# Shift and scale of the first norm made by TensorE, a block of 128 channels at a time, among the products of the first chunk

## The chip, the cores and the metric

The kernel runs on one core of one Trainium2 chip. The metric is the device time of one execution in microseconds. Three runs of the kernel before gave 1728.87, 1730.22 and 1730.78 us; the median is 1730.22 us. The execution that was profiled took 1729.32 us, and its span from the first to the last instruction is 1727.5 us.

## The reference, cut to what matters

One decoder layer for 512 tokens of 1024 channels, all in f32. The change concerns only its first lines:

```
mod = (silu(c) @ w_ada + b_ada).reshape(6, 1024)        # c: 1024 values, w_ada: 1024 x 6144
shift_m, scale_m, gate_m, shift_f, scale_f, gate_f = mod
h = rms_norm(x, norm_mix_gain) * (1.0 + scale_m) + shift_m
proj = h @ w_in                                          # q | k | v | p, 4096 columns
```

`rms_norm` divides x by the root of the mean of its squares over the 1024 channels. What follows (causal pooling, differential attention, gates, output projection, a second norm, and an expert stage with product keys that reads two tables of 16384 x 1024) is not touched.

## The kernel before, in words

**Layout.** Channels stand on the 128 partitions, in KT = 8 blocks of 128; the 512 tokens stand in a row. Each projection is cut into chunks of 256 output columns (`CHUNKS`); a chunk gives two tiles (m = 0, 1) of 128 x 512. Every product is made of three fp32r matmuls (`mm3`, L559 to L561): weights and activations are split into a high and a low part, and high x high, high x low and low x high are added up in a bank. For chunk n, ScalarE writes the high part of the weights (`whi_make`, L884), VectorE or GpSimd subtracts to get the low part (`wlo_make` L1247, `wlo_first` L1849).

**Order of the work.** Each engine has its own program, written out by hand, and the engines meet at semaphores. SyncE issues the loads from one queue in the order of `STREAM`: first the eight megabytes of `w_ada` that belong to shift_m and scale_m, each into a buffer of its own (`ada_raw`, items 0 to 7), with x (`xT`, 2 MB) behind the first of them; then the chunks' weights (1 MB each) through a ring of three slots (`raw`), with the rest of `w_ada` woven in.

**The front, up to the first chunk.** VectorE multiplies and adds the pieces of `w_ada` with silu(c) into a row sum, `acc_ada`, for shift and for scale: 16 operations of 128 x 1024, two for each megabyte (`ada_chunk`, L1220 and L1222). Each partition then holds the partial sum of its own channels. TensorE adds over the partitions and turns the row into columns: eight matmuls with one moving column each (`ada_columns`, L583), once for shift and once for scale. VectorE adds the bias (`ada_finish`, L1234) and forms `scaleA`.

Beside this, ScalarE squares x (L902), TensorE sums the squares over the channels with eight matmuls against a matrix of ones (`mean`, L571), ScalarE takes the root (L895, after a load of its table) and VectorE the reciprocal (L1280).

Then for each block k VectorE writes `tmp` (L1310), ScalarE the high part of h (L908), VectorE the low part (L1289), and TensorE multiplies block k into both tiles of chunk 0 (the branch `n == 0`, L744 to L758); the low part of the weights of tile 1 is used in eight matmuls at the end (L755). Chunk 1 follows, and from there the chunks run one after the other.

**After the front.** The chunks run to about 550 us, the expert stage streams one table through TensorE and gathers rows from both to the end. All of it is started by the work before it; nothing is set by a clock.

Of the kernel before, what the change touches and what calls it, by code (L numbers as in the profile page):

```python
# [6 lines left out]
P = 128  # L7
# [96 lines left out]
ADA_BEFORE_X = 1  # L104
# [101 lines left out]
def layer(nc, consts, chans, rows, xT_d, pos_d, subk_d, ada_d, wdram, downT, down, up, x1d, gated, out):  # L206
# [4 lines left out]
    with ExitStack() as ctx:  # L211
# [19 lines left out]
        def small(name, shape, dt=f32):  # L231
# [37 lines left out]
                   for n, kb in enumerate((68, 76, 84, 92, 116, 124, 181, 189))]  # L269
# [114 lines left out]
        sq_ready = sem("sq_ready")  # L384
        mean_ready = sem("mean_ready")
# [170 lines left out]
        def _(pe):  # L556
# [137 lines left out]
            t = 0  # L694
            for n, (stage, c) in enumerate(CHUNKS):
                if n == 1:
                    pe.wait_ge(const_in, 16)
# [23 lines left out]
                if n >= QUERY_B:  # L721
                    raw_arrived(pe, AT["w", n])
                else:
                    pe.wait_ge(hi_ready, n + 1)
                    if n == 0:
                        pe.wait_ge(lo_half, 1)
                    else:
                        pe.wait_ge(lo_ready, n + 1)
# [15 lines left out]
                elif n == 0:  # L744
                    for k in range(KT):
                        pe.wait_ge(alo_ready, N_OP["norm1"] + k + 1)
                        last = mm3(bank[:, BANK[t], :], wh[:, k, 0:P], wl[:, k, 0:P], ah[:, k, :], al[:, k, :],
                                   k == 0, k == KT - 1)
                        if k == KT - 1:
                            last.then_inc(tile_ready, 1)  # L750
                        pe.matmul(bank[:, BANK[t + 1], :], wh[:, k, P:CH], ah[:, k, :], start=(k == 0), stop=False)
                        pe.matmul(bank[:, BANK[t + 1], :], wh[:, k, P:CH], al[:, k, :], start=False, stop=False)
                    pe.wait_ge(lo_ready, 1)
                    for k in range(KT):
                        last = pe.matmul(bank[:, BANK[t + 1], :], wl[:, k, P:CH], ah[:, k, :], start=False,  # L755
                                         stop=(k == KT - 1))
                    last.then_inc(tile_ready, 1)
                    t += 2  # L758
# [22 lines left out]
                else:  # L781
                    for m in range(2):
                        free_bank(t)
                        for k in range(KT):
# [92 lines left out]
        def _(act):  # L877
# [23 lines left out]
            for k in range(KT):  # L901
# [307 lines left out]
        def _(dve):  # L1209
# [28 lines left out]
            def wlo_make(n):  # L1238
# [3 lines left out]
                if n == 0:  # L1242
                    dve.tensor_tensor(wlo[:, 0, :, P:CH], raw_w(0)[:, :, P:CH], whi[:, 0].bitcast(f32)[:, :, P:CH],
                                      ALU.subtract).then_inc(lo_ready, 1)
                    dve.wait_ge(lo_half, 1)
                    return
# [56 lines left out]
            dve.drain()  # L1303

            dve.scalar_tensor_tensor(scaleA[:, :], modc[:, KT:2 * KT], 1.0, chan[:, K_GMIX:K_GMIX + KT],
                                     ALU.add, ALU.mult)
            dve.drain()
            for k in range(KT + 1):
                if k < KT:
                    dve.scalar_tensor_tensor(tmp1[:, k, :], xT[:, k, :], scaleA[:, k:k + 1], rms1[:, :],  # L1310
                                             ALU.mult, ALU.mult).then_inc(part_ready, 1)
                if k:
                    lo_part(hT_lo[:, k - 1, :], tmp1[:, k - 1, :], hT_hi[:, k - 1, :], k, modc[:, k - 1:k])
            dve.sem_inc(root_used, 1)
# [523 lines left out]
        def _(pool):  # L1838
# [132 lines left out]
```

## Time and profile before

| what | value |
|---|---|
| median of 3 runs | 1730.22 us |
| profiled execution | 1729.32 us, span 1727.5 us |
| TensorE (PE) busy | 1604.2 us, 93% of the span |
| its weight loads (PEld) | 1175.7 us, 68% |
| VectorE (DVE) busy | 1266.0 us, 73% |
| ScalarE (ACT), GpSimd (POOL) busy | 536.4 us, 675.1 us |
| mean granted clock of TensorE | 0.970 |

Busy time of an engine over the whole span says little about one stage. The change lies in the first 53 us, so the rows below are mostly of that stretch, taken from a timeline: start, duration, engine, line, operation, output and inputs, shape, count, and in brackets how long the engine had been idle and what released it. A matmul on full f32 operands leaves two records in the trace, one on fp32r operands leaves one. The granted clock is given as a share of 2.4 GHz: 1.00 or 0.50.

### The profile page before, as it was taken

To read this page: it belongs to the slowest core of one execution; us is meant where nothing else is said; L and a number is where in the kernel's file an instruction comes from. 1 tells how busy PE (TensorE), PEld (TensorE's weight loads), DVE (VectorE), ACT (ScalarE), POOL (GpSimd) and SP (SyncE) were. 2 spreads that over 40 slices of the span, in tenths; PEclk is the share of its full clock that TensorE was granted. 3 is DMA by queue.
4 is the path that set the end of the run, shared out by engine and by line. 5 is a ranking of instruction groups with operands and counts; after the bars stand their busy time and mean duration, and the time that the engine had idled before them with its cause. 6 is when DMAs were issued, how large, how long until landed. Compare 5 with 4: busy or idle time off the path is not lost.

```text
span 1727.5 us, 20418 instructions
## 1 busy us (share of the span) xinstructions
PE 1604.2 (93%) x6936; PEld 1175.7 (68%) x6936; DVE 1266.0 (73%) x2419; ACT 536.4 (31%) x1347; POOL 675.1 (39%) x590
## 2 busy tenths in 40 slices
PE   4998999998998999999977999998999998999963
PEld 2887877776886998888866988997444443444421
DVE  6776556778466687999996888999566665676687
ACT  3432245454623612111115888876000000000000
POOL 0000121110002604534575666666744544456464
PEclk8999999999999999999988999999999999999997
DMA  8424422235332438999998999999999999999997
GB/s 334 182 87 160 151 67 78 79 102 195 143 113 86 172 122 299 376 342 351 391 335 327 382 393 392 391 390 379 360 409 409 409 409 411 409 410 409 409 411 283
DMA packets 126280, 499.18 MB, mean 289 GB/s; under 512 B 15456, under 2 KB 15840, under 8 KB 115808
## 3 DMA queue, kind: packets, MB, share of 16 engines
q0 software_dynamic: 75776, 269.52, 40.3%
q1 hardware_dynamic: 50400, 228.35, 34.5%
q8 instruction: 56, 0.92, 0.2%
q14 instruction: 48, 0.39, 0.1%
HBM read 492.04 MB, written 4.72 MB: 288 GB/s over the span
## 4 chain that ended last, share of the span: by engine, by line
DVE 30%; DMA 29%; PE 25%; POOL 5%; issue 4%; ACT 3%; DVEq 3%; SPq 0%; ACTq 0%
DMA ring<-in_up,idx 22%; DVE ring L1587 9%; DMA ring<-in_down,idx 7%; PE bank L559 6%; PE bank L560 5%; PE bank L561 5%; POOL ring L1841 5%; PE bank L848 4%; DVE accum L1830 2%; DVE acc_ada L1222 2%; PE bank L835 1%; ACT whi L884 1%; DVE wlo L1247 1%; DVE hot L1694 1%; DVEq L1256 1%
## 5 line engine op out<-in xcount | busy, mean ns | idle before, releaser
L848 PE MATMUL bank<-h2T,stream 128*128 128x256 f32 x2048 | 457.4, 382 | 9.6 <-ACTq L1178 9.6
L861 PE MATMUL bank<-stream,wmat 128*128 128x512 f32 x1024 | 444.7, 597 | 11.5 <-DMA stream<-in_up 7.0
L1830 DVE SCALAR_TENSOR_TENSOR accum<-ring,share,accum 128x1024 f32<-128x1024 f32 x245 | 314.6, 1284 | 178.1 <-DMA ring<-in_up,idx 175.1
L1841 POOL DMA_INDIRECT ring<-in_down,idx x256 | 326.4, 1275 | 271.0 <-DVE pre L1587 185.3
L848 PEld LDWEIGHTS bank<-h2T,stream 128*128 128x128 f32 x2048 | 387.2, 192 | 60.7 <-issue 9.9
L861 PEld LDWEIGHTS bank<-stream,wmat 128*128 128x128 f32 x1024 | 196.1, 192 | 259.4 <-issue 246.9
L1841 POOL DMA_INDIRECT ring<-in_up,idx x256 | 274.9, 1074 | 230.8 <-DVE accum L1830 191.7
L1587 DVE CUSTOM_DVE_ANT_0 ring<-ring,h2row 128x1024 f32<-128x1024 f32 x256 | 307.7, 1220 | 40.0 <-DMA ring<-in_down,idx 36.1
L559 PE MATMUL bank<-hT_hi,whi 128*128 128x512 f32 (+1 forms) x504 | 190.1, 377 | 12.1 <-DVE hT_lo L1289 9.5
L561 PE MATMUL bank<-hT_hi,wlo 128*128 128x512 f32 (+1 forms) x504 | 185.1, 367 | 0.0
L560 PE MATMUL bank<-hT_lo,whi 128*128 128x512 f32 (+1 forms) x504 | 184.8, 367 | 0.0
L1856 POOL TENSOR_TENSOR wlo<-raw,whi 128x2048 fp32r<-128x2048 f32 x8 | 37.2, 4655 | 203.2 <-ACT whi L884 203.2
L559 PEld LDWEIGHTS bank<-hT_hi,whi 128*128 128x128 f32 x504 | 97.0, 192 | 27.4 <-issue 11.9
L1190 ACT ACTIVATE junk<-yrow 128x1024 f32<-128x1024 f32 x4 | 4.2, 1056 | 347.4 <-DVE yrow L1805 347.4
L1247 DVE TENSOR_TENSOR wlo<-raw,whi 128x2048 fp32r<-128x2048 f32 x36 | 82.5, 2291 | 39.4 <-ACT whi L884 38.3
L884 ACT ACTIVATE whi<-raw 128x2048 fp32r<-128x2048 f32 x45 | 86.0, 1912 | 75.6 <-PE bank L561 71.5
L561 PEld LDWEIGHTS bank<-hT_hi,wlo 128*128 128x128 f32 x504 | 96.7, 192 | 15.8
L1149 ACT ACTIVATE h2T<-h2T,gT,gneg 128x128 f32<-128x128 f32 x256 | 105.5, 482 | 5.0 <-issue 0.3
L560 PEld LDWEIGHTS bank<-hT_lo,whi 128*128 128x128 f32 x504 | 97.1, 193 | 14.1 <-issue 0.2
L1177 ACT ACTIVATE wmat<-bank 128x256 f32<-128x256 f32 (+21 forms) x128 | 42.1, 329 | 190.7 <-PE bank L848 190.6
L1870 POOL DMA_DIRECT2D q_rot<-q_raw x64 | 33.1, 524 | 134.7 <-ACT q_raw L984 134.4
L1144 ACT ACTIVATE h2T<-cst,ijT 128x128 f32<-128x128 f32 x256 | 81.8, 390 | 6.5
(228 smaller groups left out, 1833.6 us busy)
## 6 DMA issues: line engine op xcount, KB each, us to landing
stream<-in_downT SPq DMA_DIRECT2D x128, 512.0 KB, 6.7
stream<-in_up SPq DMA_DIRECT2D x128, 512.0 KB, 6.8
raw<-in_ada SPq DMA_DIRECT2D x16, 1024.0 KB, 4.9
raw<-in_w_query SPq DMA_DIRECT2D x16, 1024.0 KB, 4.9
ada_raw<-in_ada SPq DMA_DIRECT2D x8, 1024.0 KB, 16.5
raw<-in_w_xp SPq DMA_DIRECT2D x4, 1024.0 KB, 12.8
raw<-in_w_gateA SPq DMA_DIRECT2D x4, 1024.0 KB, 4.8
raw<-in_w_branchP SPq DMA_DIRECT2D x4, 1024.0 KB, 4.8
```

Source lines behind the costliest of these rows:

```text
L559: pe.matmul(dst, lhi, rhi, start=first, stop=False)
L560: pe.matmul(dst, lhi, rlo, start=False, stop=False)
L561: return pe.matmul(dst, llo, rhi, start=False, stop=last)
L848: last = pe.matmul(bank[:, 4 + i % 2, 0:DT], stream[:, i % RING, k * P:(k + 1) * P], h2T[:, k, GB * P:S], start=(k == 0), stop=(k == KT - 1))
L861: last = pe.matmul(bank[:, 2 * tb + half, :], wmat[:, i, tb * P:(tb + 1) * P], stream[:, (ET + i) % RING, half * S:(half + 1) * S], start= ...
L884: act.activation(whi[:, n % 2], raw_w(n), ACT.Copy).then_inc(hi_ready, 1)
L1144: act.activation(h2T[:, 4 * par + n, P:2 * P], cst[:, C_IOTA:C_IOTA + P], ACT.Abs, bias=ijT[:, b, 0, t0 + n:t0 + n + 1])
L1149: last = act.activation(h2T[:, 4 * par + n, P:2 * P], h2T[:, 4 * par + n, P:2 * P], ACT.Relu, bias=gT[:, b, t:t + 1], scale=gneg[:, b, t:t ...
L1247: dve.tensor_tensor(wlo[:, n % 2], raw_w(n), whi[:, n % 2].bitcast(f32), ALU.subtract)\
L1587: dve.tensor_tensor_reduce(out=ring[slot][:, :], in0=ring[slot][:, :], in1=h2row[:, b, :], scale=1.0, scalar=0.0, op0=ALU.mult, op1=ALU.ad ...
L1830: dve.scalar_tensor_tensor(accum[:, b, :], ring[slot][:, :], share[:, b, k:k + 1], accum[:, b, :], ALU.mult, ALU.add).then_inc(sum_done, 1)
L1841: pool.indirect_dma_start(out=ring[slot][:, :], out_offset=None, in_=table, in_offset=bass.IndirectOffsetOnAxis(ap=idx[:, b, k:k + 1], axi ...
```

## The change: what it does, and the diff

1. **Layout of the weights.** The part of `w_ada` for shift and scale is laid out by output block on the host: piece k holds, for the 128 channels of block k, all 1024 x 128 weights of shift and all of scale. Before, a piece held 256 input rows of one of the two.
2. **Loads.** x comes first, then the weights of chunk 0 (now in front of the eight pieces), then the pieces; the small constants come behind the weights of chunk 1. `ada_raw` lies at other addresses.
3. **Multiplication.** The 16 operations of VectorE and the 16 matmuls of `ada_columns` go. In their place TensorE makes each block in 16 matmuls with one moving column (`ada_block`: 8 for shift, 8 for scale), adding up in the bank. VectorE adds the bias for two columns and forms one column of `scaleA` (`ada_columns_in`).
4. **Order.** TensorE's order is written out in `FRONT`: blocks a0, a1, a2, then the product of block 0 (p0), a3, p1, and so on. A product is now 6 matmuls for both tiles (`first_product`), without the eight at the end.
5. **Squares.** ScalarE squares five blocks, VectorE three. VectorE adds them in pairs, and TensorE sums four blocks where it summed eight. The table for the root is loaded ahead by a small operation.
6. **Low parts.** GpSimd makes both halves of chunk 0's low weights and one half of chunk 1's; VectorE makes one half of chunk 1's.

```diff
+FRONT = ("a0", "a1", "a2", "p0", "a3", "p1", "a4", "p2", "a5", "p3", "a6", "p4", "a7", "p5", "p6", "p7")
+SQUARE_PAIRS = ((0, 1), (2, 3), (5, 6), (4, 7))
...
             sp.dma_start(chan[:, :], chans).then_inc(chan_in, 16)
+            sp.dma_start(xT[:, :, :], xT_d).then_inc(xT_in, 16)
+            sp.dma_start(raw_at(OUTSIDE), wdram["xp"][0]).then_inc(raw_in[0], 16)
             for n, item in enumerate(STREAM):
...
-                sp.dma_start(raw_at(n), src).then_inc(ada_in[n] if m < 0 else raw_in[m % RAW_SLOTS], 16)
-                if n == ADA_BEFORE_X - 1:
-                    sp.dma_start(xT[:, :, :], xT_d).then_inc(xT_in, 16)
-                if n == OUTSIDE:
+                if m:
+                    sp.dma_start(raw_at(n), src).then_inc(ada_in[n] if m < 0 else raw_in[m % RAW_SLOTS], 16)
+                if n == OUTSIDE + 1:
...
+            def ada_block(k):
+                raw_arrived(pe, k)
+                if k == 0:
+                    pe.wait_ge(cact_ready, 1)
+                if k >= 2:
+                    pe.wait_ge(cols_read, k - 1)
+                for sec in range(2):
+                    for kk in range(KT):
+                        last = pe.matmul(bank[:, 5 + 2 * (k % 2), 3 * P + sec:3 * P + sec + 1],
+                                         ada_raw[k][:, (2 * kk + sec) * P:(2 * kk + sec + 1) * P],
+                                         cact[:, kk:kk + 1], start=(kk == 0), stop=(kk == KT - 1))
+                last.then_inc(cols_ready, 1)
+
+            def first_product(k):
+                wh, wl, ah, al = whi[:, 0], wlo[:, 0], hT_hi, hT_lo
+                if k == 0:
+                    pe.wait_ge(hi_ready, 1)
+                pe.wait_ge(alo_ready, N_OP["norm1"] + k + 1)
+                for m in range(2):
+                    if k == 0:
+                        pe.wait_ge(lo_half, m + 1)
+                    last = mm3(bank[:, BANK[m], :], wh[:, k, m * P:(m + 1) * P], wl[:, k, m * P:(m + 1) * P],
+                               ah[:, k, :], al[:, k, :], k == 0, k == KT - 1)
...
             pe.wait_ge(ones_ready, 1)
-            pe.wait_ge(sq_ready, 8)
-            mean([sq1[:, k, :] for k in range(KT)])
-            ada_columns(0)
-            ada_columns(1)
+            for n, (k, _) in enumerate(SQUARE_PAIRS):
+                pe.wait_ge(pair_ready, n + 1)
+                last = pe.matmul(bank[:, 6, :], ones[:, :], sq1[:, k, :], start=(n == 0),
+                                 stop=(n == len(SQUARE_PAIRS) - 1))
+            last.then_inc(mean_ready, 1)
+            for what in FRONT:
+                (ada_block if what[0] == "a" else first_product)(int(what[1:]))
+            pe.sem_inc(ada_col, 2)
...
-            for k in range(KT):
+            for k in range(5):
                 act.activation(sq1[:, k, :], xT[:, k, :], ACT.Square).then_inc(sq_ready, 1)
             act.wait_ge(ones_ready, 1)
+            act.activation(lamt[:, 0:1], eps_t[:, :], ACT.Sqrt)
             root(0, 1.0 / D)
...
-            dve.wait_ge(cact_ready, 1)
-            for j in range(2):
-                for r in range(4):
-                    ada_chunk(j, r)
-            inverse_root(0)
-            ada_finish(0)
-            ada_finish(1)
+            dve.wait_ge(xT_in, 16)
+            for k in (5, 6, 7):
+                dve.tensor_tensor(sq1[:, k, :], xT[:, k, :], xT[:, k, :], ALU.mult)
+            dve.drain()
+            for n, (one, two) in enumerate(SQUARE_PAIRS):
+                dve.wait_ge(sq_ready, (2, 4, 4, 5)[n])
+                dve.tensor_tensor(sq1[:, one, :], sq1[:, one, :], sq1[:, two, :], ALU.add).then_inc(pair_ready, 1)
+            inverse_root(0)
+            def ada_columns_in(k):
...
+                dve.wait_ge(cols_ready, k + 1)
+                dve.tensor_tensor(both, bank[:, 5 + 2 * (k % 2), 3 * P:3 * P + 2], bias, ALU.add).then_inc(cols_read, 1)
+                dve.drain()
+                dve.scalar_tensor_tensor(scaleA[:, k:k + 1], modc[:, KT + k:KT + k + 1], 1.0,
+                                         chan[:, K_GMIX + k:K_GMIX + k + 1], ALU.add, ALU.mult)
...
             for k in range(KT + 1):
                 if k < KT:
+                    ada_columns_in(k)
                     dve.scalar_tensor_tensor(tmp1[:, k, :], xT[:, k, :], scaleA[:, k:k + 1], rms1[:, :],
                                              ALU.mult, ALU.mult).then_inc(part_ready, 1)
                 if k:
                     lo_part(hT_lo[:, k - 1, :], tmp1[:, k - 1, :], hT_hi[:, k - 1, :], k, modc[:, k - 1:k])
...
-                pool.wait_ge(hi_ready, 1)
-                pool.tensor_tensor(wlo[:, 0, :, 0:P], raw_w(0)[:, :, 0:P], whi[:, 0].bitcast(f32)[:, :, 0:P],
-                                   ALU.subtract).then_inc(lo_half, 1)
+                for n, m in ((0, 0), (0, 1), (1, 1)):
+                    pool.wait_ge(hi_ready, n + 1)
+                    half = slice(m * P, (m + 1) * P)
+                    pool.tensor_tensor(wlo[:, n, :, half], raw_w(n)[:, :, half], whi[:, n].bitcast(f32)[:, :, half],
+                                       ALU.subtract).then_inc(lo_half, 1)
```

## Rows read from the trace of the kernel before

**Rows 1.** The page: span, and TensorE's busy tenths in 40 slices.

```profile
span 1727.5 us, 20418 instructions
PE   4998999998998999999977999998999998999963
```

**Rows 2.** Timeline of all engines, start of the program up to x and weights.

```profile
6.71 0.75 DVE L1220 TENSOR_SCALAR acc_ada<-ada_raw,cact 128x1024 f32<-128x1024 f32 x1 [5.69 <-DMA ada_raw<-in_ada]
11.53 4.27 ACT L902 ACTIVATE sq<-xT 128x512 f32<-128x512 f32 x8 [8.82 <-DMA xT<-in_xT]
14.01 8.08 DVE L1222 SCALAR_TENSOR_TENSOR acc_ada<-ada_raw,cact,acc_ada 128x1024 f32<-128x1024 f32 x6 [5.18 <-DMA ada_raw<-in_ada]
...
26.98 0.69 ACT L895 ACTIVATE rms<-bank,eps_t 128x512 f32<-128x512 f32 x1
31.42 1.91 ACT L884 ACTIVATE whi<-raw 128x2048 fp32r<-128x2048 f32 x1 [3.76 <-DMA raw<-in_w_xp]
32.60 3.35 DVE L1280 RECIPROCAL rms<-rms 128x512 f32<-128x512 f32 x1
33.41 2.36 POOL L1849 TENSOR_TENSOR wlo<-raw,whi 128x1024 fp32r<-128x1024 f32 x1 [32.96 <-ACT whi L884]
```

**Rows 3.** Timeline of TensorE alone, from its first matmul to chunk 1.

```profile
15.94 9.66 PE L571 MATMUL bank<-sq,ones 128*128 128x512 f32 x16 [15.94 <-ACT sq L902]
25.43 1.84 PE L583 MATMUL bank<-ones,acc_ada 128*128 128x1 f32 x16
32.57 3.58 PE L583 MATMUL bank<-ones,acc_ada 128*128 128x1 f32 x16 [5.29 <-DVEq L1227]
39.14 0.77 PE L559 MATMUL bank<-hT_hi,whi 128*128 128x512 f32 x1 [3.00 <-DVE hT_lo L1289]
39.70 0.63 PE L560 MATMUL bank<-hT_lo,whi 128*128 128x512 f32 x1
...
44.82 0.47 PE L751 MATMUL bank<-hT_hi,whi 128*128 128x512 f32 x1
...
52.85 0.39 PE L559 MATMUL bank<-hT_hi,whi 128*128 128x512 f32 x1
```

**Rows 4.** Timeline of the weight loads of the mean and of the one-column matmuls.

```profile
16.93 0.34 PEld L571 LDWEIGHTS bank<-sq,ones 128*128 128x128 f32 x1 [0.52 <-issue]
17.78 0.34 PEld L571 LDWEIGHTS bank<-sq,ones 128*128 128x128 f32 x1 [0.52 <-issue]
...
21.14 0.19 PEld L571 LDWEIGHTS bank<-sq,ones 128*128 128x128 f32 x1 [0.47 <-issue]
...
25.43 1.75 PEld L583 LDWEIGHTS bank<-ones,acc_ada 128*128 128x128 f32 x15 [0.24 <-issue]
32.57 3.49 PEld L583 LDWEIGHTS bank<-ones,acc_ada 128*128 128x128 f32 x16 [5.38 <-DVEq L1227]
```

**Rows 5.** Stretches: length, then busy us of PE, PEld, DVE, ACT, POOL; PEclk; DMA share; GB/s.

```profile
27.00:28.00 1.00, 0.28 (x3) 0.19 (x2) 0.93 (x2) 0.67 (x1) 0.00 (x0) 0.95 0.99 410
44.00:45.00 1.00, 1.00 (x4) 0.81 (x3) 1.00 (x3) 0.40 (x2) 0.00 (x0) 0.51 0.00 0
414.00:416.00 2.00, 2.00 (x20) 1.96 (x19) 1.91 (x3) 0.48 (x1) 0.00 (x0) 1.00 0.93 385
417.00:418.00 1.00, 0.00 (x0) 0.00 (x0) 1.00 (x1) 0.35 (x1) 0.00 (x0) 0.51 0.00 0
1680.00:1682.00 2.00, 0.30 (x1) 0.00 (x0) 1.83 (x3) 0.00 (x0) 1.70 (x2) 1.00 1.02 408
```

**Rows 6.** DVE groups of 60 to 140 us: busy, mean ns, idle before.

```profile
L1379 DVE TENSOR_TENSOR pool_w<-xpT 128x512 f32<-128x512 f32 x8 | 5.5, 690 | 0.6
```

**Rows 7.** What TensorE waited for from 52 to 700 us: total, times, longest.

```profile
PE bank L620 <- DVE comb L1417: 6.5, 9, 1.9
PE bank L559 <- DVE hT_lo L1289: 6.5, 1, 6.5
PE bank L559 <- ACT mergedP L1085: 2.4, 1, 2.4
```

More of the change, by code:

```diff
@@ L268, in layer @@
         ada_raw = [place(f"ada_raw{n}", [P, 2 * D], f32, kb)
-                   for n, kb in enumerate((68, 76, 84, 92, 116, 124, 181, 189))]
+                   for n, kb in enumerate((44, 60, 116, 124, 148, 181, 189, 197))]
         raw = place("raw", [P, RAW_SLOTS, KT * CH], f32, 12)
@@ L384, in layer @@
         sq_ready = sem("sq_ready")
+        pair_ready = sem("pair_ready")
+        cols_ready = sem("cols_ready")
+        cols_read = sem("cols_read")
         mean_ready = sem("mean_ready")
@@ L585, in ada_columns @@
                 last.then_inc(ada_col, 1)
-            pe.wait_ge(ones_ready, 1)
-            pe.wait_ge(sq_ready, 8)
-            mean([sq1[:, k, :] for k in range(KT)])
-            ada_columns(0)
-            ada_columns(1)
+            def ada_block(k):
[20 more added lines that the diff above has]
+                               ah[:, k, :], al[:, k, :], k == 0, k == KT - 1)
+                    if k == KT - 1:
+                        last.then_inc(tile_ready, 1)
+            pe.wait_ge(ones_ready, 1)
+            for n, (k, _) in enumerate(SQUARE_PAIRS):
[6 more added lines that the diff above has]
+            pe.sem_inc(ada_col, 2)
             ada_before = {}
@@ L692, in score @@
                 return t + 1
-            t = 0
+            t = 2
             for n, (stage, c) in enumerate(CHUNKS):
+                if n == 0:
+                    continue
                 if n == 1:
@@ L743, in _ @@
                             t += 1
-                elif n == 0:
-                    for k in range(KT):
[L746 to L758, printed above, removed]
                 elif stage == "v":
@@ L783, in _ @@
                         free_bank(t)
+                        if n == 1 and m == 1:
+                            pe.wait_ge(lo_half, 3)
                         for k in range(KT):
@@ L1242, in wlo_make @@
                 if n == 0:
-                    dve.tensor_tensor(wlo[:, 0, :, P:CH], raw_w(0)[:, :, P:CH], whi[:, 0].bitcast(f32)[:, :, P:CH],
+                    dve.wait_ge(lo_half, 2)
+                    dve.sem_inc(lo_ready, 1)
+                    return
+                if n == 1:
+                    dve.tensor_tensor(wlo[:, 1, :, 0:P], raw_w(1)[:, :, 0:P], whi[:, 1].bitcast(f32)[:, :, 0:P],
                                       ALU.subtract).then_inc(lo_ready, 1)
-                    dve.wait_ge(lo_half, 1)
+                    dve.wait_ge(lo_half, 3)
                     return
@@ L1295, in _ @@
             dve.sem_inc(ones_ready, 1)
-            dve.wait_ge(cact_ready, 1)
-            for j in range(2):
-                for r in range(4):
-                    ada_chunk(j, r)
-            inverse_root(0)
-            ada_finish(0)
-            ada_finish(1)
[L1303 to L1307, printed above, removed]
+            dve.wait_ge(xT_in, 16)
[7 more added lines that the diff above has]
+            def ada_columns_in(k):
+                both = modc[:, 0:2 * KT].rearrange("p (j k) -> p j k", k=KT)[:, :, k]
+                bias = chan[:, K_BADA:K_BADA + 2 * KT].rearrange("p (j k) -> p j k", k=KT)[:, :, k]
+                dve.wait_ge(cols_ready, k + 1)
[3 more added lines that the diff above has]
+                                         chan[:, K_GMIX + k:K_GMIX + k + 1], ALU.add, ALU.mult)
+                dve.drain()
+            dve.wait_ge(cact_ready, 1)
             for k in range(KT + 1):
                 if k < KT:
+                    ada_columns_in(k)
                     dve.scalar_tensor_tensor(tmp1[:, k, :], xT[:, k, :], scaleA[:, k:k + 1], rms1[:, :],
@@ L1313, in _ @@
                     lo_part(hT_lo[:, k - 1, :], tmp1[:, k - 1, :], hT_hi[:, k - 1, :], k, modc[:, k - 1:k])
+            dve.sem_inc(ada_acc, 2)
+            dve.sem_inc(ada_done, 2)
             dve.sem_inc(root_used, 1)
@@ L1945 @@
         "subk": np.ascontiguousarray(a["peer_sub_keys"][0].transpose(2, 0, 1)),
-        "ada": np.ascontiguousarray(a["w_ada"][0].reshape(4, 2, P, 6, D).transpose(3, 0, 2, 1, 4)
-                                    .reshape(6, 4, P, 2 * D)),
+        "ada": np.ascontiguousarray(np.concatenate([
+            a["w_ada"][0][:, :2 * D].reshape(KT, P, 2, KT, P).transpose(3, 1, 0, 2, 4).reshape(2, 4, P, 2 * D),
+            a["w_ada"][0][:, 2 * D:].reshape(4, 2, P, 4, D).transpose(3, 0, 2, 1, 4).reshape(4, 4, P, 2 * D)])),
         "w_xp": chunks(w_in[:, 3 * D:]), "w_q": chunks(w_in[:, :D]), "w_k": chunks(w_in[:, D:2 * D]),
```

7 lines of the change are left out of this document (1 added, 6 removed).

## The prediction

> **What bounds the kernel now.** I read the page first, for the span of 1727.5 us and the busy tenths of TensorE [rows 1]. After the first of the 40 slices they are mostly 8 or 9, so a front that ends later pushes a full TensorE ahead of it. Then I read what TensorE waits for between 52 and 700 us: single stalls of 6.5 and 2.4 us and a few short ones [rows 7], all on work that itself follows from earlier work. Nothing there waits for an absolute time, so I let a shift of the end of the front reach the end of the kernel one to one.
>
> Then the timeline of the first 53 us. The first megabyte of `w_ada` is there at 6.71, x (2 MB behind it) at 11.53, the next megabyte at 14.01, and the eleventh and last, the weights of chunk 0, at 31.42 [rows 2]: 2.4 to 2.5 us for each megabyte. VectorE is the bound before the first product: it waits 5.18 us for the second megabyte, then works without a gap from 14.01 to 32.5 through the rest of its 16 row operations, and takes 3.35 us for the reciprocal from 32.60 [rows 2]. TensorE has only the mean (9.66 us from 15.94) and two batches of eight one-column matmuls (1.84 us at 25.43, 3.58 us at 32.57); the first product starts at 39.14 and chunk 1 at 52.85 [rows 3]. The reader should see that VectorE works and TensorE is nearly empty, and, just as important, what the few one-column matmuls cost. The point to compare is the start of chunk 1, 52.85 us.
>
> **The change, part by part.**
>
> *Loads.* Only the order changes. x is first and is there at 11.53 less one megabyte of 2.4, about 9.1; the chunk's weights about 11.5; piece k about 14.0 + 2.5 k; the last about 31.4, where the eleventh megabyte lands now [rows 2]. These arrivals are no bound if TensorE comes to each piece later, which it does below.
>
> *Squares and mean.* ScalarE does eight squares in 4.27 us [rows 2], so five take 2.7 us: 9.1 to 11.8. VectorE squares three blocks beside it and adds a pair. The nearest row is 0.69 us for a 128 x 512 addition [rows 6], so the first pair is ready at 9.1 + 4 x 0.7 + drains, about 12.0. TensorE then needs four f32 matmuls of two records each. At the low level records start 0.85 us apart (16.93, 17.78) and the loads shorten at 21.14, 5.2 us after the first matmul [rows 3, 4]: that is TensorE at 1.2 GHz, then at 2.4 GHz. Eight records take 6.8 us at the low level; with the rise after 5.2 us I take 6.0, to 18.0. The other pairs are added in 0.7 us each, beneath matmuls of 1.7 us. The root takes 0.69 and the reciprocal 3.35 [rows 2]; with the table loaded ahead, VectorE has the reciprocal at about 22.4. Bounds: 17.3 to 18.8 for the end of the mean.
>
> *High and low parts of chunk 0.* Its weights are there, so ScalarE's 1.91 us and GpSimd's two halves of 2.36 us [rows 2] end near 25.5, beneath the blocks a0 to a2.
>
> *The blocks on TensorE.* This is the large term. `ada_block` issues 16 matmuls of f32, 128 x 128 weights, one moving column, the same form as L583. Eight of those took 3.58 us at the low level and 1.84 us at the high one, and their weight loads fill that time: 3.49 us for 16 and 1.75 for 15 [rows 3, 4]. So the single column costs nothing and the weights everything. The change has 8 blocks x 16 = 128 matmuls, sixteen such batches: 16 x 3.49 = 55.8 us at 1.2 GHz, or 16 x 1.75 = 28.0 us at 2.4 GHz. Before, TensorE had two batches. The 16 operations that VectorE loses had run beside an idle TensorE; the work now lies on the engine that also has the products.
>
> The Trainium skill ("TensorE: Matmul & The Clock Gate", section on LDWEIGHTS) gives a load as its columns over 1.2 GHz, whatever the array's clock: an estimate from it is 107 ns for 128 columns, 256 records, 27 us in all. The trace agrees at the high level and disagrees at the low one, where a load takes 218 ns; by the page the slow case below would not exist.
>
> *The products.* 8 x 6 = 48 fp32r matmuls, as many as now. They start 0.43 us apart at the low level: the twelve between 39.70 and 44.82 [rows 3]. At the high level a record on fp32r takes half of this, 0.22 to 0.23. So 20.5 us or 10.9 us.
>
> *The clock.* All 77 us of this can go at either level. The granted clock fell near 27.9, right after the first batch of one-column matmuls, with TensorE idle only since 27.27, and near 417 after a stretch from 414 to 416 in which TensorE was busy for all 2.00 us, 1.84 of it such a batch [rows 3, 5]. Near the end of the kernel it stayed at 1.00 though TensorE was busy 0.30 of 2.00 us, with matmuls 512 wide around the gap [rows 5]. So the batches do not hold the clock up as wide matmuls do. In the changed kernel a0, a1 and a2 follow each other for over 10 us with one column each. I expect the fall about 3 us after the mean (27.9 - 25.4 in one case, 417 - 414.1 in the other). The rises of the trace came 5.2 us after dense matmuls began (15.94 to 21.14) and 5.8 us (39.14 to 44.98) [rows 3, 4, 5]; the product blocks, 2.56 us each between blocks of 7.0, are shorter than both, so I take no rise among them.
>
> *Waits that come in.* a2 to a7 wait until VectorE has read the block two before. Behind that wait stands all of TensorE; but VectorE is free from 22.4 and reads a block within 0.3 us, while each block lasts at least 3.5, so it costs nothing; if VectorE were late by a block it would cost up to 3 us once. A product k waits for the low part k, which stands behind `ada_columns_in(k + 1)` on VectorE, and so behind block a(k+1). In `FRONT` each product up to p5 has that block well before it. After a7, p6 and p7 need 2.2 and 2.8 us of VectorE and ScalarE (now 3.0 from the end of the one-column matmuls, 36.15, to the first product [rows 3]). At the low level p5 and p6 cover this; at the high level 0.9 us shows. Chunk 1 needs its high part (1.91) and half a subtraction behind the last high part of h: a7 + 5.3 us. The last block's products at the low level end at a7 + 6.5 and cover it.
>
> *The sum.* Mean ends 18.0. Blocks 55.8 and products 20.5 at the low level give 94.3. Minus 3.0, since about 3 us at the high level do 6 us of low work. Minus 1.25 at the end: p5, p6 and p7 are 7.7 us of dense matmuls, the clock rises after 5.2, and the remaining 2.5 takes half. That gives 90.0 for the start of chunk 1 against 52.85: +37.2 us. VectorE, next in line behind, ends its last low part 2.8 us after a7, 3.6 us before TensorE ends, and has 2.3 us less of subtractions behind it, so it is no later than TensorE. The profiled execution would go from 1729.32 to 1766.5; that execution is 0.9 us under the median of the runs, so the forecast is 1767.
>
> Bounds of this case: with 5 us at the high level after the mean, and rises in the mean and after p5 that come 1.5 us sooner than those of the trace (my allowance), 17.3 + 76.3 - 5.0 - 2.0 = 86.6, or +33.8. With neither and the mean wholly at the low level, 18.8 + 76.3 = 95.1, or +42.3. So 1763 to 1773.
>
> **The rivals.**
>
> *The clock stays high (B).* TensorE has no gap from the mean on. For it: the low level came each time with at least 0.6 us of idle TensorE as well. Against it: rows 5 as read above. Time: 18.0 + 28.0 + 5 x 1.36 = 52.8 at the end of a7, + 5.3 to chunk 1, 58.1: +5.3 us, 1735.5. The Trainium skill (the same page, "HAM oscillation") lays a fall to gaps of idle time between matmuls; by that rule there is none here and B holds. The trace agrees only in that the idle stretch and the batch came together.
>
> *The clock comes and goes (D).* The five product blocks between, or a favourable alternation, lift it for part of the way: between a quarter and three quarters of the 32 us between B and A, +13 to +29, say 1751. For it: a product block fills a good part of the time that a rise took at the least. Against it: both rises of the rows came more than 5 us into dense work, and a product block lasts 2.56.
>
> *Not slower: the arrival decides (C).* If a block took TensorE only one record for each matmul, eight would cost 0.9 us: 18.0 + 14.4 + 6.8 + 5.3 = 44.5, or -8.4 us, 1722; the last piece's arrival at 31.4 is the floor beneath it. The point from which it decides is a batch of eight under 1.4 us at the high level: then the front ends before 52.85. For it: VectorE's 18 us row work really goes, and x is there 2.4 us sooner. Against it: the batch has the same shape as L583, 16 records, 1.84 us at its best [rows 3].
>
> **How the numbers follow.** A 0.72, D 0.10, B 0.12, C 0.03, and 0.03 for a shift that is swallowed later by a stall that I let pass [rows 7]. The likeliest is A: 1767. The range runs from 1748, which takes in most of D, to 1774, the upper bound of A with a little for the unmeasured VectorE squares; it leaves out B and C. About 0.2% (3.5 us) is what a measurement can tell from no change. B at +5.3 still counts as slower, so slower is A, D and B with a part of the rest, 0.95; same 0.02; faster 0.03.
>
> **What would show it.** In the profile after: one-column matmuls, 256 records, beginning near 18 us; a granted clock of 0.50 from about 21 until the last products; a batch of 32 records in 7.0 us each; the products between in 2.6 us; `ada_raw` never waited for; chunk 1 near 90 us; everything behind it as before, moved by 37 us. I am wrong if the clock stays at 1.00 through a1 and a2 (then B), if a block takes clearly less than 3.5 us (then C), or if the end of the kernel does not move with chunk 1.

## The result, and the profile after

| | before | changed |
|---|---|---|
| median | 1729.59 us (4 runs, 1728.87 to 1730.78) | 1764.63 us (4 runs, 1759.33 to 1767.09) |
| ratio | | 1.0198, 95% interval 1.0171 to 1.0225 |
| profiled execution | 1729.32 us, span 1727.5 | 1767.09 us, span 1765.3 |
| start of chunk 1 | 52.85 us | 87.38 us |

The kernel became 35 us slower. The forecast was 1767, with a range from 1748 to 1774.

The timeline of TensorE in the changed kernel shows the front whole (L623 is the mean, L601 the blocks, L564 to L566 the products; start, duration, count; in brackets how long it was idle). It answers to [rows 3].

```profile
11.75 5.96 PE L623 MATMUL bank<-sq,ones 128*128 128x512 f32 x8 [11.75 <-DVE sq L1330]
17.55 18.44 PE L601 MATMUL bank<-cact,ada_raw 128*128 128x1 f32 x96
35.84 0.77 PE L564 MATMUL bank<-hT_hi,whi 128*128 128x512 f32 x1
...
38.55 6.82 PE L601 MATMUL bank<-cact,ada_raw 128*128 128x1 f32 x32
45.23 0.77 PE L564 MATMUL bank<-hT_hi,whi 128*128 128x512 f32 x1
...
64.00 0.77 PE L564 MATMUL bank<-hT_hi,whi 128*128 128x512 f32 x1
...
66.71 4.04 PE L601 MATMUL bank<-cact,ada_raw 128*128 128x1 f32 x32
70.61 0.48 PE L564 MATMUL bank<-hT_hi,whi 128*128 128x512 f32 x1
...
73.02 6.83 PE L601 MATMUL bank<-cact,ada_raw 128*128 128x1 f32 x32
79.70 0.77 PE L564 MATMUL bank<-hT_hi,whi 128*128 128x512 f32 x1
...
87.38 0.47 PE L564 MATMUL bank<-hT_hi,whi 128*128 128x512 f32 x1 [1.01 <-DVE wlo L1271]
```

From 11.75 to 86.4 us TensorE has no gap. A block of 32 records starts its product 6.68 us later (38.55 to 45.23): 0.209 us a record. One block, a6, takes 3.90 (66.71 to 70.61). The stretches show why; they answer to [rows 5] (length, then busy us of PE, PEld, DVE, ACT, POOL, the granted clock, DMA share, GB/s).

```profile
17.00:19.00 2.00, 2.00 (x16) 1.64 (x15) 0.53 (x1) 1.25 (x2) 0.00 (x0) 1.00 0.99 418
19.00:21.00 2.00, 2.00 (x15) 2.00 (x14) 2.00 (x1) 1.23 (x1) 0.69 (x1) 0.69 1.03 430
21.00:23.00 2.00, 2.00 (x11) 2.00 (x11) 1.28 (x3) 0.00 (x0) 2.00 (x2) 0.50 1.00 418
...
66.00:68.00 2.00, 2.00 (x12) 1.81 (x10) 0.09 (x1) 0.18 (x1) 0.00 (x0) 0.61 0.00 0
68.00:70.00 2.00, 2.00 (x20) 2.00 (x19) 0.00 (x0) 0.00 (x0) 0.00 (x0) 1.00 0.00 0
```

With TensorE busy throughout, the clock falls near 19.8, two microseconds into the one-column matmuls, and stays at 1.2 GHz. It rises near 67.6, 0.9 us into a6 and behind the wide product block p3, is high for the rest of a6, falls again at 71.0 in p4, and rises near 84.6, within the last products.

VectorE, the bound before, now waits 43.2 us for TensorE's blocks:

```profile
DVE modc L1338 <- PE bank L601: 43.2, 8, 7.5
```

Behind the front the shift is carried on. The first row is the table stage on TensorE of the changed kernel, the second the stage behind it, the third that same stage in the kernel before (first and last start are the two numbers after the durations):

```profile
L871 PE MATMUL bank<-h2T,stream x2048: 379/379/767, 709.5 to 1237.6; 128*128 128x256 f32 x187
L884 PE MATMUL bank<-stream,wmat x1024: 592/592/1222, 1244.4 to 1694.7; 128*128 128x512 f32 x171
```

```profile
L861 PE MATMUL bank<-stream,wmat x1024: 592/592/1222, 1207.1 to 1658.2; 128*128 128x512 f32 x171
```

The table stage started at 676.5 before and starts at 709.5 now: +33.0. The stage behind it starts at 1244.4 instead of 1207.1: +37.3. Between them lie 534.9 us instead of 530.6. In the profiles of the experiments below, whose code there is the same, this distance was 526.7 us (e6) to 536.6 us (e8), so I count the 4.3 us to that spread and not to the change.

### The profile page after: what moved, and what is told of

Same layout as the page of the kernel before. It is cut to its first block, busy times and chain, and to the rows that moved or that the text cites. A ratio compares the mean times of both kernels' runs of the same rounds, so it can differ in the third digit from the quotient of the medians.

```text
span 1765.3 us, 20862 instructions
## 1 busy us (share of the span) xinstructions
PE 1649.4 (93%) x7152; PEld 1220.3 (69%) x7152; DVE 1254.0 (71%) x2422; ACT 535.9 (30%) x1345; POOL 669.3 (38%) x592
## 4 chain that ended last, share of the span: by engine, by line
DMA 31%; DVE 29%; PE 24%; POOL 5%; issue 4%; ACT 4%; DVEq 3%; ACTq 0%; SPq 0%
DMA ring<-in_up,idx 21%; DMA ring<-in_down,idx 9%; DVE ring L1627 9%; PE bank L564 5%; POOL ring L1881 5%; PE bank L565 5%; PE bank L566 5%; PE bank L601 3%; DVE accum L1870 2%; PE bank L871 1%; ACT whi L907 1%; DVE wlo L1275 1%; DVE hot L1734 1%; DVEq L1284 1%; DVE att_max L1442 1%
## 5 line engine op out<-in xcount | busy, mean ns | idle before, releaser
L1881 POOL DMA_INDIRECT ring<-in_down,idx x256 | 319.7, 1249 | 281.3 <-DVE pre L1627 196.3
L1881 POOL DMA_INDIRECT ring<-in_up,idx x256 | 271.2, 1059 | 237.8 <-DVE accum L1870 199.1
L564 PE MATMUL bank<-hT_hi,whi 128*128 128x512 f32 (+1 forms) x512 | 196.4, 384 | 10.1 <-DVE hT_lo L1317 6.5
L565 PE MATMUL bank<-hT_lo,whi 128*128 128x512 f32 (+1 forms) x512 | 190.7, 372 | 0.0
L566 PE MATMUL bank<-hT_hi,wlo 128*128 128x512 f32 (+1 forms) x512 | 190.7, 372 | 0.0
L564 PEld LDWEIGHTS bank<-hT_hi,whi 128*128 128x128 f32 x512 | 100.0, 195 | 26.2 <-issue 10.3
L566 PEld LDWEIGHTS bank<-hT_hi,wlo 128*128 128x128 f32 x512 | 99.9, 195 | 16.6
```

What stands on the lines that cost most here:

```text
L564: pe.matmul(dst, lhi, rhi, start=first, stop=False)
L565: pe.matmul(dst, lhi, rlo, start=False, stop=False)
L566: return pe.matmul(dst, llo, rhi, start=False, stop=last)
L1881: pool.indirect_dma_start(out=ring[slot][:, :], out_offset=None, in_=table, in_offset=bass.IndirectOffsetOnAxis(ap=idx[:, b, k:k + 1], axi ...
```

## The experiments

My theory was that two things make the loss: the blocks put 256 weight loads on TensorE's path, and one-column matmuls let its clock fall, which doubles that price. The rivals were that the order and its waits make it, and that the low level alone does. Ratios are to the kernel before, run on the same chip in the same job.

### e1: the weights move instead of the one column

```diff
-                for sec in range(2):
-                    for kk in range(KT):
-                        last = pe.matmul(bank[:, 5 + 2 * (k % 2), 3 * P + sec:3 * P + sec + 1],
-                                         ada_raw[k][:, (2 * kk + sec) * P:(2 * kk + sec + 1) * P],
-                                         cact[:, kk:kk + 1], start=(kk == 0), stop=(kk == KT - 1))
+                for kk in range(KT):
+                    last = pe.matmul(bank[:, 5 + 2 * (k % 2), 0:2 * P], rep[:, kk, :],
+                                     ada_raw[k][:, 2 * kk * P:2 * (kk + 1) * P],
+                                     start=(kk == 0), stop=(kk == KT - 1))
...
```

`rep` is silu(c), each value repeated over 128 columns by VectorE. VectorE also picks the wanted columns out of the bank for each block, with a product and a sum over the columns.

> The changed kernel with operands swapped in the blocks: silu(c) of one block of 128 inputs, repeated over 128 columns, is the stationary operand and the weights move, 256 columns at once (8 matmuls a block in place of 16); VectorE picks the columns out with the identity. TensorE's passes are as many as before: 16 records of 256 columns a block. Theory 1 (the one-column form lets the clock fall, and the level makes most of the loss): blocks take about 3.4 us each, the clock stays at 1.00 through the front, chunk 1 starts near 58 to 59 us instead of 87.4, and the kernel takes 1735 to 1739 us. Rival (the new order and its waits make the loss): blocks may be shorter but chunk 1 stays near 85 us and the time near 1764 us.

Measured: 1739.52 us, ratio 1.0060 (1.0041 to 1.0079). Timeline of TensorE and two long stretches of it:

```profile
17.44 10.52 PE L603 MATMUL bank<-ada_raw,rep 128*128 128x256 f32 x48
28.88 0.47 PE L567 MATMUL bank<-hT_hi,whi 128*128 128x512 f32 x1 [0.92 <-issue]
...
30.34 3.62 PE L603 MATMUL bank<-ada_raw,rep 128*128 128x256 f32 x16
33.60 0.58 PE L567 MATMUL bank<-hT_hi,whi 128*128 128x512 f32 x1
...
56.31 0.50 PE L567 MATMUL bank<-hT_hi,whi 128*128 128x512 f32 x1 [1.61 <-DVE hT_lo L1319]
...
61.82 0.47 PE L567 MATMUL bank<-hT_hi,whi 128*128 128x512 f32 x1 [2.46 <-DVE wlo L1273]
```

```profile
18.00:36.00 18.00, 17.08 (x79) 14.56 (x78) 13.76 (x23) 4.29 (x5) 4.66 (x2) 1.00 1.02 417
36.00:54.00 18.00, 18.00 (x83) 15.51 (x83) 9.21 (x22) 2.89 (x4) 0.00 (x0) 1.00 0.08 32
```

The same sums in the same order, with wide moving operands: the clock is 1.00 in both stretches, a block's product starts 3.26 us after the block (30.34 to 33.60) in place of 6.68, and chunk 1 starts 25.6 us sooner than in the changed kernel. The order and its waits are still there, so they do not make the 35 us. The new form is also a little cheaper by itself: the rows of e3 put a one-column block at the high level at 3.43 us (an estimate, 32 x 0.107), so about 1.4 us of the 25.6 are the form and not the clock. Chunk 1 is 3 us later than I expected. TensorE, now faster, waits three times: 0.92 us before p0, 1.61 before p6, and 2.46 before chunk 1, the last for the reason that e6 shows.

### e2: all blocks first, then all products

```diff
-FRONT = ("a0", "a1", "a2", "p0", "a3", "p1", "a4", "p2", "a5", "p3", "a6", "p4", "a7", "p5", "p6", "p7")
+FRONT = ("a0", "a1", "a2", "a3", "a4", "a5", "a6", "a7", "p0", "p1", "p2", "p3", "p4", "p5", "p6", "p7")
```

> The changed kernel with all eight blocks first and all eight products behind them. The work on TensorE is the same. Theory 1 (level of the clock): the blocks run at 218 ns a load, the products are one dense stretch of 20.5 us at the low level in which the clock rises after some 5 us, so they take about 13 us; chunk 1 starts at 84 to 86 us, 1760 to 1764 us in all. Rival (interleaving hides work that would show otherwise): chunk 1 gets later, by the chain of VectorE and ScalarE that no longer runs between blocks, 5 us or more.

Measured: 1759.87 us, ratio 1.0172 (1.0133 to 1.0211).

```profile
17.64 52.50 PE L601 MATMUL bank<-cact,ada_raw 128*128 128x1 f32 x256
70.00 0.77 PE L564 MATMUL bank<-hT_hi,whi 128*128 128x512 f32 x1
...
74.41 0.47 PE L565 MATMUL bank<-hT_lo,whi 128*128 128x512 f32 x1
...
83.15 0.39 PE L564 MATMUL bank<-hT_hi,whi 128*128 128x512 f32 x1
```

The 256 records take 52.4 us on end. The dense products lift the clock 4.4 us after they begin, and chunk 1 starts at 83.15, with no wait of TensorE before it. The rival, that interleaving hides work, falls. Whether the order is worth anything is open: the changed kernel starts chunk 1 at 87.38 in one execution and at 81.68 in another (e9), on both sides of 83.15, and the intervals of the times overlap. It is in any case not the 35 us.

### e3: most of the sum for shift left out

```diff
-                    for kk in range(KT):
+                    for kk in range(KT if sec else 1):
...
```

> The changed kernel with seven of the eight matmuls left out of the sum for shift in each block (the sum for scale is whole): 9 matmuls a block instead of 16. Theory 1 (weight loads at 0.22 us a record set the front): 56 matmuls of two records less are 24 us at the low level; the product blocks are a larger part, so the clock may rise more often; chunk 1 near 60 us or earlier, total 1733 to 1740 us. Rival (waits set the front): less than 10 us gained.

Measured: 1738.83 us, ratio 1.0056 (1.0034 to 1.0078). The kernel leaves out seven eighths of the sum for shift: a block is 9 matmuls, 18 records.

```profile
30.93 2.31 PE L601 MATMUL bank<-cact,ada_raw 128*128 128x1 f32 x18
33.10 0.48 PE L564 MATMUL bank<-hT_hi,whi 128*128 128x512 f32 x1
...
34.57 2.07 PE L601 MATMUL bank<-cact,ada_raw 128*128 128x1 f32 x18
36.50 0.47 PE L564 MATMUL bank<-hT_hi,whi 128*128 128x512 f32 x1
...
54.32 0.47 PE L564 MATMUL bank<-hT_hi,whi 128*128 128x512 f32 x1 [2.48 <-DVE wlo L1271]
```

```profile
34.00:50.00 16.00, 15.49 (x105) 13.82 (x104) 8.99 (x20) 4.76 (x6) 0.00 (x0) 1.00 0.22 85
```

Chunk 1 starts 33 us sooner than in the changed kernel, more than the 24 us of loads taken out at the low level: with shorter blocks the clock comes back near 31.5 us and stays at 1.00 through the alternation, though the blocks still have one moving column. A block's product starts 1.93 us after the block (34.57 to 36.50): 0.107 us a record, the price of this form at the high level. The total, with routing computed from other values, gained less than the front (26 us), and I do not read more from it.

### e5: the rest of the change alone

Squares, pairs, table and the order of the loads as in the change; shift and scale as row operations of VectorE, as before.

```diff
             dve.sem_inc(ones_ready, 1)
+            dve.wait_ge(xT_in, 16)
+            for k in (5, 6, 7):
+                dve.tensor_tensor(sq1[:, k, :], xT[:, k, :], xT[:, k, :], ALU.mult)
...
             dve.wait_ge(cact_ready, 1)
             for j in range(2):
                 for r in range(4):
                     ada_chunk(j, r)
...
```

> The kernel before with only the other parts of the change: x and the weights of chunk 0 loaded first, squares shared by ScalarE and VectorE and added in pairs, table loaded ahead; shift and scale stay row operations of VectorE. Theory 1 (these parts are worth nothing by themselves since VectorE is the bound): VectorE has 4.4 us more of squares before the row operations and they start near 13.5 us, end near 35, chunk 1 at 54 to 56 us, total +1 to +3 us over the kernel before. Rival (the earlier x and mean bring something of their own): faster than before.

Measured: 1735.50 us, ratio 1.0043 (1.0028 to 1.0058). TensorE, then one row of VectorE:

```profile
37.08 3.58 PE L585 MATMUL bank<-ones,acc_ada 128*128 128x1 f32 x16 [6.80 <-DVEq L1233]
43.65 0.77 PE L561 MATMUL bank<-hT_hi,whi 128*128 128x512 f32 x1 [3.00 <-DVE hT_lo L1295]
...
56.51 0.47 PE L561 MATMUL bank<-hT_hi,whi 128*128 128x512 f32 x1
```

```profile
16.42 10.19 DVE L1228 SCALAR_TENSOR_TENSOR acc_ada<-ada_raw,cact,acc_ada 128x1024 f32<-128x1024 f32 x6 [0.27 <-DMA ada_raw<-in_ada]
```

The second batch of columns starts at 37.08 instead of 32.57 and chunk 1 at 56.51: 3.7 us later. The rival falls: an earlier x and an earlier mean bring nothing while VectorE's row operations set the end. I had not expected 2.1 us of it: six row operations take 10.19 us where they took 8.08 [rows 2]. One of them lasts 3.40 us instead of 1.28, while GpSimd makes its half of the low weights (20.48 to 22.82), which in the kernel before lay beside the reciprocal; e6 comes back to it. The timed loss, 5 to 10 us by the interval, is more than the front shows; the profiled execution was the fastest of ten (1730.6). What the others lose beyond the front is open.

### e4: the kernel before with TensorE kept at work

```diff
             ada_columns(0)
+            for _ in range(WARM_A):
+                pe.matmul(bank[:, 4, :], ones[:, :], sq1[:, 0, :], start=True, stop=True)
             ada_columns(1)
+            for _ in range(WARM_B):
+                pe.matmul(bank[:, 4, :], ones[:, :], sq1[:, 0, :], start=True, stop=True)
```

`WARM_A` is 6 and `WARM_B` is 3.

> The kernel before with nine wide f32 matmuls on TensorE whose result nobody reads: six behind the first batch of one-column matmuls, three behind the second. Theory 1: they hold the clock at 1.00 from 27 us on, the second batch takes 1.84 instead of 3.58 us and the first products start 0.23 us apart, but VectorE (reciprocal to 35.9, then 1.33 us for each block) sets the pace, so chunk 1 starts only 0.5 to 1 us earlier and the total does not change measurably. Rival (the low clock in the front of the kernel before costs its 5 us in full): 3 to 4.6 us faster.

Measured: 1729.33 us, ratio 0.9992 (0.9975 to 1.0010).

```profile
32.57 1.84 PE L584 MATMUL bank<-ones,acc_ada 128*128 128x1 f32 x16
34.27 2.82 PE L596 MATMUL bank<-sq,ones 128*128 128x512 f32 x6
...
51.75 0.47 PE L560 MATMUL bank<-hT_hi,whi 128*128 128x512 f32 x1 [0.64 <-DVE wlo L1252]
```

Wide matmuls between the batches hold the clock (1.00 from 18 to 54 us), the second batch takes 1.84 us in place of 3.58 [rows 3], and chunk 1 gains 1.1 us. So a low level costs almost nothing where VectorE is the bound. It cost some 25 us in the changed kernel (worked out behind the experiments) because the work had been moved onto the engine whose clock it lowers. Neither cause alone makes the 35 us.

### e6: chunk 1's low weights by VectorE alone

```diff
-                for n, m in ((0, 0), (0, 1), (1, 1)):
+                for n, m in ((0, 0), (0, 1)):
...
-                    dve.tensor_tensor(wlo[:, 1, :, 0:P], raw_w(1)[:, :, 0:P], whi[:, 1].bitcast(f32)[:, :, 0:P],
-                                      ALU.subtract).then_inc(lo_ready, 1)
-                    dve.wait_ge(lo_half, 3)
+                    dve.tensor_tensor(wlo[:, 1], raw_w(1), whi[:, 1].bitcast(f32), ALU.subtract).then_inc(lo_ready, 1)
...
```

> The changed kernel with the low part of chunk 1's weights made by VectorE alone (2048 columns, one instruction) instead of half by GpSimd and half by VectorE. In the changed kernel VectorE's half takes 3.44 us where the same shape took 1.22 before, and ends 1.1 us after GpSimd's half of 2.39. Theory 1 (VectorE's subtraction of two operands waits for the whole GpSimd instruction beside it): alone it takes 2.29 us, TensorE's wait of 1.0 us before chunk 1 goes. Rival (the time is set by something else in that place, such as the load of the weights): it takes more than 3 us again and the wait stays.

Measured: a single execution, 1759.15 us, which is too little to tell a gain in the total. The first two rows are from the changed kernel (VectorE's half, GpSimd's half), the third is VectorE's whole in e6.

```profile
83.79 3.44 DVE L1271 TENSOR_TENSOR wlo<-raw,whi 128x1024 fp32r<-128x1024 f32 x1 [0.72 <-ACT whi L907]
```

```profile
83.76 2.39 POOL L1891 TENSOR_TENSOR wlo<-raw,whi 128x1024 fp32r<-128x1024 f32 x1 [58.81 <-ACT whi L907]
```

```profile
84.01 2.29 DVE L1269 TENSOR_TENSOR wlo<-raw,whi 128x2048 fp32r<-128x2048 f32 x1 [0.71 <-ACT whi L905]
```

Both halves are issued together. VectorE's lasts until 87.23, 1.08 us after GpSimd's is over at 86.15: about its own length (the shape took 1.22 before). Alone, VectorE makes the whole in 2.29, and TensorE's wait before chunk 1 is gone. The two did not share, one waited for the other. The Trainium skill says so ("SBUF — State Buffer", section on the two separate sides): GpSimd and a VectorE operation with two SBUF inputs take the shared ports in turn, each for its whole instruction. The trace agrees, with 3.44 us for 1.22.

It shows in other places too. In the changed kernel GpSimd's first two halves run from 20.31 to 24.95, and an operation of VectorE on 128 x 1 elements, 0.16 us for every other block, lasts until they are over:

```profile
22.70 2.27 DVE L1340 SCALAR_TENSOR_TENSOR scaleA<-modc,chan 128x1 f32<-128x1 f32 x1
```

There it costs nothing, since TensorE is busy until 35.84. In e1 and e7 the like operation takes 1.98 us, VectorE works without a gap from there to the first low part of h, and TensorE stands idle for 0.92 us before p0; without the delay that idle time would not be there, by the times of these rows, but no run took it out.

### e7: e1 without the end of the front

ScalarE makes chunk 1's high part behind block 4; VectorE makes its low part between blocks, GpSimd none of it:

```diff
+                if k == 4:
+                    whi_make(1)
...
+                if k in (6, 7):
+                    dve.wait_ge(hi_ready, 2)
+                    half = slice((k - 6) * P, (k - 5) * P)
+                    dve.tensor_tensor(wlo[:, 1, :, half], raw_w(1)[:, :, half], whi[:, 1].bitcast(f32)[:, :, half],
+                                      ALU.subtract)
...
```

> e1 (weights moving, clock high) with the split of chunk 1's weights taken out of the end of the front: ScalarE makes the high part behind block 4, VectorE makes the low part in two halves behind blocks 5 and 6, GpSimd has no part of it. Theory 1 (with a high clock only TensorE's work is left: 27.3 us of blocks and 10.9 us of products behind the mean): chunk 1 starts at 58 to 59 us, with no wait ahead of it, 2.5 to 3.5 us earlier than in e1, and the kernel is 5 to 8 us slower than before. Rival (VectorE, which now has 2.4 us more between blocks, holds the products up): chunk 1 at 60 us or later.

Measured: 1736.21 us, ratio 1.0027 (1.0010 to 1.0044). Timeline of TensorE:

```profile
56.30 0.50 PE L567 MATMUL bank<-hT_hi,whi 128*128 128x512 f32 x1 [1.61 <-DVE hT_lo L1317]
...
59.60 0.39 PE L567 MATMUL bank<-hT_hi,whi 128*128 128x512 f32 x1
```

Chunk 1 starts at 59.60, directly behind the last product, 2.2 us sooner than in e1. That is less than the least I expected (2.5), and between my theory (58 to 59) and the rival (60 or later): the waits of 0.92 us before p0 and 1.61 before p6 are still there, as in e1. So the +6.8 us in the front are the blocks' price at the high clock with 2.5 us of idle TensorE in it.

### e8: rows and wide blocks mixed

Blocks 0 and 3 by VectorE in rows, the rest as in e7; four banks in turn for the blocks, and an order with more blocks ahead (a0 to a4 before p0).

```diff
+BY_ROWS = (0, 3)
...
+            def ada_rows(k):
+                n = BY_ROWS.index(k)
+                raw_arrived(dve, k)
+                acc = sq1[:, 2 * n + 1, 0:2 * P]
+                for kk in range(KT):
+                    src = ada_raw[k][:, 2 * kk * P:2 * (kk + 1) * P]
+                    if kk == 0:
+                        dve.tensor_scalar(acc, src, cact[:, 0:1], None, ALU.mult)
+                    else:
+                        dve.scalar_tensor_tensor(acc, src, cact[:, kk:kk + 1], acc, ALU.mult, ALU.add)
...
```

> A mixture: blocks 0 and 3 of shift and scale are made by VectorE in rows (8 operations of 128 x 256) with two one-column matmuls each, the other six by TensorE with the weights moving as in e1; the high part of chunk 1's weights is made behind block 4, its low part by VectorE between blocks, GpSimd has no part of it. TensorE then has 6 x 3.4 + 1 + 10.9 us behind the mean, VectorE about 31 us behind 17.9. Theory 1 (the front is bound by the sum of work on TensorE and VectorE at the high clock, and by nothing else): chunk 1 starts at 50 to 52 us, and the kernel is 1 to 3 us faster than before. Rival (the handing over between the engines costs more than it saves): chunk 1 at 54 us or later, slower than before.

Measured: 1733.91 us, ratio 1.0017 (1.0003 to 1.0031), in 12 runs. TensorE at block 3 and at chunk 1, then VectorE, where block 3's first row operation stands behind GpSimd:

```profile
28.55 0.79 PE L606 MATMUL bank<-ones,sq 128*128 128x1 f32 x4 [2.12 <-DVEq L1355]
...
56.59 0.39 PE L569 MATMUL bank<-hT_hi,whi 128*128 128x512 f32 x1
```

```profile
22.27 2.28 DVE L1352 TENSOR_SCALAR sq<-ada_raw,cact 128x256 f32<-128x256 f32 x1
```

It missed my 50 to 52, and the gain; the rival held (54 or later, and slower). Block 0 is ready 1.7 us and block 3 some 2 us after TensorE wants them; the first row operation of block 3 takes 2.28 us where block 0's took 0.35, until GpSimd's low parts end. This is the nearest that the new layout came to the kernel before, and it is not faster.

### e9: the changed kernel again

> The changed kernel once more, unchanged, for its spread: its four runs lay between 1759.3 and 1767.1 us. Theory 1 (whether a product block lifts the clock depends on where it falls against the times at which the level can change): the profile shows another block or other blocks at the full clock than block a6, or none, each worth about 3 us, and the runs spread over more than 5 us. Rival (the lift of a6 is a fixed property of the order): a6 at the full clock again and nothing else.

Measured: 1763.94 us (4 runs, 1759.68 to 1768.85), ratio 1.0203 (1.0174 to 1.0231).

```profile
17.66 15.42 PE L601 MATMUL bank<-cact,ada_raw 128*128 128x1 f32 x96
...
54.42 6.82 PE L601 MATMUL bank<-cact,ada_raw 128*128 128x1 f32 x32
...
63.81 3.80 PE L601 MATMUL bank<-cact,ada_raw 128*128 128x1 f32 x32
...
70.08 4.07 PE L601 MATMUL bank<-cact,ada_raw 128*128 128x1 f32 x32
...
81.68 0.47 PE L564 MATMUL bank<-hT_hi,whi 128*128 128x512 f32 x1 [1.69 <-DVE wlo L1271]
```

The same program: the first three blocks take 15.4 us instead of 18.4, since the clock falls 5.5 us behind the mean (at 23.2) and not 2.2, and a6 and a7 are both mostly at the high clock (in e6, whose front is the same up to there, it was a5 alone). Chunk 1 starts 5.7 us sooner, and the span is 5.2 us shorter. So where the clock falls and rises differs between executions, and each such difference is worth about 3 us; the rival, that the lift of a6 is fixed, falls. It does not follow that the spread of the runs, 8 and 9 us, comes from it: in the eight runs of both sets the mean clock does go from 0.959 in the two slowest to 0.962 and 0.963 in the two fastest, but the kernel before, which has no such blocks, spreads by 13 us in the 23 runs beside these.

## Why the prediction was right

The sign, the mechanism and the size held: chunk 1 was forecast at 90.0 and came at 87.38, the total at 1767 and came at 1764.6. That the profiled execution, at 1767.09, met the 1766.5 forecast for it so closely is luck: its front was 2.6 us better than forecast and the rest 3.3 us longer. In e9 the same program starts chunk 1 at 81.68, below the 86.6 that I had given as the least, while its time stays in the range. Step by step:

- **Loads, squares, mean:** the mean ended at 17.55 for 18.0, x was there at 8.93 for 9.1. VectorE's squares took 0.63 us where I used 0.69. No piece of `ada_raw` was waited for.
- **Blocks, the large term:** 256 records at 0.209 us are 53.5 us for my 55.8. I had divided the length of a batch by its records, and that length runs to the end of the last one, while only the distance from start to start repeats. The 28.0 for the high level is near what e3's rows give, 256 x 0.107 = 27.4 us (an estimate); in e1's form the blocks took 8 x 3.26 = 26.1.
- **Products:** 2.71 us a block at the low level for 2.56.
- **Clock:** the fall came 2.2 us behind the mean for 3. "I take no rise among them" failed: the clock rose at 67.6, behind p3 (64.00 to 66.71), and in e9 two blocks gained. This is rival D, to which I gave 0.10 as a case of its own; it is a part of each of the three profiled executions with this front (here, e6, e9), worth 3 to 6 us, not 8 to 24. From two rises after more than 5 us of dense work I had inferred that shorter work does not do it; the rows only show how long it took in two cases. Here a6 came 3.1 us shorter than forecast, more than the 2.6 us by which chunk 1 came early; the other differences (mean -0.5, a0 to a2 +0.4, the other four blocks -1.2, products +0.5, the distance to chunk 1 behind them +1.2) nearly cancel.
- **Waits that come in:** no wait of a2 to a7, as forecast. I had costed chunk 1's half subtraction by the row of the same shape, 1.22, and it took 3.44 beside GpSimd. Nothing in [rows 2] shows it: GpSimd's half there lies beside the reciprocal, which kept its 3.35 us. The price was 1.0 us here, 1.7 in e9 and 2.5 in e1, where TensorE had less left to cover it.
- **Shift to the end, one to one:** +34.5 at chunk 1, +33.0 where the table stage starts (VectorE is further ahead of TensorE behind the front than before, which would explain it, but no run tested that), then +37.3 and +37.8 by the spread of the table stage.
- **Rival B** (58.1 for chunk 1 at the high clock, +5.3) is nearly e7: 59.60, +6.8. The idea behind it, that a busy TensorE keeps its clock, falls: it was busy without a gap when the clock fell at 19.8. The Trainium skill ("TensorE: Matmul & The Clock Gate", "HAM oscillation") ties the fall to idle gaps; here the measurement decides against taking that as the only way.
- **Rival C** falls with the count of records: 32 for a block of 16 matmuls.

Of the 34.5 us in the front, 6.8 are there in e7 too, at the high clock (2.5 of them idle TensorE), and 1.0 is the wait in front of chunk 1. Of the other 26.7 about 1.4 are the cheaper form of e7's blocks, so some 25 us are the low level. This is an estimate. A second one is in line with it: TensorE was at the low level for 61.4 us of this front (19.8 to 67.6 and 71.0 to 84.6), of which the high level would save half, 30.7, and some of that would come back as waits for VectorE, as in e7. No run holds the clock up in the changed kernel and leaves its one-column blocks as they are, so this share is worked out and not measured by itself.

## What to carry to other kernels

Before a sum is moved from VectorE to TensorE, count its weight loads: here a matmul with one moving column cost its weight load, twice for f32, and 128 of them are 27 us at the high clock and 53 at the low one. Long runs of one-column matmuls did not hold the clock up here; if they must be many, let the wide operand move. And on the path, do not start a VectorE operation with two SBUF inputs beside a GpSimd one on SBUF, for one simply follows the other.

## What the runs showed of the hardware that was not expected

- TensorE, busy without a gap, was set to 1.2 GHz 2.2 us after starting one-column matmuls (5.5 us in e9), and held 1.00 through alternating blocks of 256 moving columns (e1), and through one-column blocks of 18 records between the same products (e3).
- Behind a product block of 2.71 us at the low level the clock rose in some places and not in others, and in different ones from execution to execution: a6, a5 (e6), or a6 and a7 (e9) gained.
- VectorE's operation with two SBUF inputs waits for a whole GpSimd instruction (3.44 us for 1.2 of work, 2.27 for 0.16, and 3.40 for 1.28 in e5); a `tensor_scalar` in f32 did too (2.28 us for 0.35, e8), while the reciprocal did not (3.35 us with GpSimd beside it, and 3.35 without in e5).
